# Where two pairs of modulation products and a table load stand in the norm transitions of a two-layer hybrid transformer

## The reference, cut to what matters

```python
def _rmsnorm(x, g):
    y = xf * lax.rsqrt(jnp.mean(xf * xf, axis=-1, keepdims=True) + EPS)
    return (y * g.astype(jnp.float32)).astype(x.dtype)

def _adaln(cond, w, b):
    return (jax.nn.silu(cond) @ w + b).reshape(cond.shape[0], 3 * N_SUB, D_MODEL)

def _modulate(x, g, mod, j):
    return _rmsnorm(x, g) * (1 + mod[:, 3 * j + 1, None]) + mod[:, 3 * j, None]

def _ffn_half(h, mod, j, g, w1, w3, w2):
    u = _modulate(h, g, mod, j)
    return h + 0.5 * mod[:, 3 * j + 2, None] * ((jax.nn.silu(u @ w1) * (u @ w3)) @ w2)
```

## Time and profile before

| what | us |
|---|---|
| median of 3 runs (lowest, highest) | 3353.94 (3353.17, 3354.42) |
| the profiled execution | 3349.25 |
| its span, first to last instruction | 3347.5 |
| PE busy in the span | 3190.4 (95%) |
| DVE busy | 1740.0 (52%) |
| ACT busy | 1406.5 (42%) |
| POOL busy | 124.1 (4%) |

### The profile page before, as it was taken

One profiled execution on the slowest core, in us unless ns is written; L12 is line 12 of the kernel. 1 busy time (PEld: TensorE's weight loads), 2 busy tenths in 40 slices (PEclk: granted clock), 3 DMA queues, 4 the chain that ended last, 5 costly groups with the idle time before them and its releaser, 6 DMA issues.

```text
span 3347.5 us, 51456 instructions
## 1 busy us (share of the span) xinstructions
PE 3190.4 (95%) x18766; PEld 2651.3 (79%) x18766; DVE 1740.0 (52%) x3164; ACT 1406.5 (42%) x2189; POOL 124.1 (4%) x120
## 2 busy tenths in 40 slices
PE   7999989999989899999999999999999998899898
PEld 4777768888877578777788867777788888699898
DVE  4333357777634823434333343334677775856555
ACT  4222256565434722224222242223655654654544
POOL 0000010111000000000000000000000000000000
PEclk9999999999999999999999999999899999999999
DMA  7443421111122043222432243434111113144454
GB/s 285 149 152 127 159 87 64 38 56 44 45 82 82 1 145 120 88 94 97 162 104 97 97 148 132 169 132 155 60 50 50 56 51 117 54 147 164 155 183 145
DMA packets 101261, 363.43 MB, mean 109 GB/s; under 512 B 11153, under 2 KB 12817, under 8 KB 101009
## 3 DMA queue, kind: packets, MB, share of 16 engines
q1 hardware_dynamic: 98384, 353.02, 30.9%
q10 hardware_dynamic: 2752, 8.72, 0.7%
HBM read 360.58 MB, written 1.11 MB: 108 GB/s over the span
## 4 chain that ended last, share of the span: by engine, by line
PE 85%; DVE 7%; ACT 4%; issue 3%; DMA 1%; SPq 0%; DVEq 0%; POOL 0%; POOLq 0%; ACTq 0%
PE bank L1662 67%; PE bank L1919 3%; PE bank L1917 2%; DVE wlo L1013 2%; PE bank L1687 2%; ACT whi L490 1%; PE bank L1970 1%; ACT scr L932 1%; PE bank L1978 1%; DVE h L1113 1%; PE bank L1988 1%; PE bank L1990 1%; PE bank L2125 1%; PE bank L2148 1%; PE bank L1960 1%
## 5 line engine op out<-in xcount | busy, mean ns | idle before, releaser
L1662 PE MATMUL bank<-uh,whi 128*128 128x512 f32 (+1 forms) x3008 | 1118.0, 372 | 52.9 <-ACTq L890 17.0
L1662 PE MATMUL bank<-ul,whi 128*128 128x512 f32 (+1 forms) x3008 | 1084.5, 361 | 0.0
L1662 PE MATMUL bank<-uh,wlo 128*128 128x512 f32 (+1 forms) x3008 | 1082.8, 360 | 0.5 <-DVE scr L1403 0.3
L490 ACT ACTIVATE whi<-raw 128x1024 fp32r<-128x1024 f32 x520 | 548.2, 1056 | 1209.3 <-PE bank L1662 1208.9
L1013 DVE TENSOR_TENSOR wlo<-raw,whi 128x1024 fp32r<-128x1024 f32 x520 | 642.4, 1235 | 790.5 <-ACT whi L490 789.2
L1662 PEld LDWEIGHTS bank<-uh,whi 128*128 128x128 f32 x3008 | 578.2, 192 | 160.5 <-issue 63.8
L1662 PEld LDWEIGHTS bank<-uh,wlo 128*128 128x128 f32 x3008 | 576.5, 192 | 81.8 <-DVE scr L1403 1.6
L1662 PEld LDWEIGHTS bank<-ul,whi 128*128 128x128 f32 x3008 | 578.7, 192 | 69.8 <-issue 2.2
L1662 PE MATMUL bank<-bh,whi 128*128 128x512 f32 (+1 forms) x1088 | 387.9, 357 | 1.1 <-DVE h L1113 0.8
L1662 PE MATMUL bank<-bl,whi 128*128 128x512 f32 (+1 forms) x1088 | 384.5, 353 | 0.0
L1662 PE MATMUL bank<-bh,wlo 128*128 128x512 f32 (+1 forms) x1088 | 384.4, 353 | 0.0
(11 more groups left out here) (247 smaller groups left out, 3041.3 us busy)
## 6 DMA issues: line engine op xcount, KB each, us to landing
raw<-stream SPq DMA_DIRECT2D x524, 512.0 KB, 3.3
ada_raw<-stream SPq DMA_DIRECT2D x131, 512.0 KB, 5.2
gc_row<-gc_rows ACTq DMA_DIRECT2D x16, 512.0 KB, 3.6
h<-h_in SPq DMA_DIRECT2D x1, 2048.0 KB, 10.9
m<-stream SPq DMA_DIRECT2D x4, 512.0 KB, 12.4
cst<-consts SPq DMA_DIRECT2D x1, 1104.0 KB, 12.5
scr<-stream SPq DMA_DIRECT2D x2, 512.0 KB, 16.2
out<-m SPq DMA_DIRECT2D x8, 128.0 KB, 1.8
```

Source lines behind the costliest of these rows:

```text
L490: act.activation(whi[:, j, :], raw[:, j, :], ACT.Copy).then_inc(hi_ready, 1)
L1662: last = mm(bank[j][:, c0:T], w(t, a), x[:, t, c0:T], start=n == 0, stop=n == 3 * kts - 1)
```

## The change

TensorE: in `last_products` the first pair of the leading group is issued behind panel (1, 1), the second of the last four, and the second pair between `sums_but_last` and `sum_last` instead of behind it. ScalarE: in transitions 1 to 6 the table load is issued before the wait for the residual of tile 7 and its square, instead of behind that square and the last weight split. SyncE: the load of the second pair of a leading group follows the raw load of panel 1 of its block, not of panel 2 (except for the first group, whose place is unchanged).

```diff
             if lead:
-                free = (max(b + 1, 1), 2 + k)
+                free = (b + 1, 1 + 2 * k) if b else (1, 2 + k)
             else:
                 free = (b + 2, 2 * k)
...
             def norm_rstd(n):
                 c0 = norm_conds(n)
-                log_exp()
+                if n == 0:
+                    log_exp()
                 act.wait_ge(var_ready, n + 1)
                 rsqrt(nrs[:, c0:T], nvar[:, c0:T], rstd_ready)
...
                 for i in range(2):
                     for j in range(4):
                         t = 4 * i + j
+                        if t == KT - 1:
+                            log_exp()
                         if j % 2:
                             have(act, pair_done[j // 2], G0 + i + 1)
                         else:
...
             def last_products(B0, G0, n, xh, xl, c0, kts=KT, ready=None, tile=None):
 
+                after = lead_after(n)
                 for i in range(2):
                     for j in range(4):
...
                         pair_free(G0 + i, j)
                         panel(B0 + i, j, xh, xl, c0, kts=kts, ready=ready if (i, j) == (0, 0) else None)
+                        if after is not None and (i, j) == (1, 1):
+                            ada_pair(after, 0)
                 sums_but_last(n)
-                after = lead_after(n)
-                if after is not None:
-                    ada_pair(after, 0)
-                sum_last(n)
                 if after is not None:
                     ada_pair(after, 1)
+                sum_last(n)
```

## The result

| | before | after |
|---|---|---|
| median of 22 runs (lowest, highest) | 3353.04 (3347.92, 3355.99) | 3356.98 (3355.27, 3360.58) |
| the profiled execution | 3349.25 | 3359.12 |
| its span | 3347.5 | 3357.3 |
| PE busy | 3190.4 (95%) | 3192.2 (95%) |

The ratio of the times is 1.0015, with a 95% interval of 1.0009 to 1.0022: slower by 5.0 (3.0 to 7.4). The medians lie only 3.9 apart, the means of the 22 runs each (3352.1 and 3357.2) 5.1: the runs of before fall into two groups, nine of 3347.9 to 3350.7 and thirteen of 3352.3 to 3356.0, and what parts them was not looked into. Forecast was +4.1. In the code of after the lines stand three further down: `panel` is L1665, the pair L1690, the first sum L1711, the last sum L1717, the variance L1033.

A forecast was written before the change was run, and what follows sets the result against it. The prediction took TensorE as the bound (85% of the span ends on it), time being lost where it stands still or another engines' chain sets its next matmul. 5.2 + 1.0 - 2.1 = +4.1, 3358.0 by the median; range 3351 to 3363.

The forecast's parts named there:

- the likeliest case: Transitions 1, 3, 4: last sum waits for the second pair's weights; forecast +4.1, anywhere up to +5.3, chance 0.67.
- Table load, 2.1 saved: ScalarE, load ahead of the last Square: Ln sooner by 0.31 in transitions 1, 3, 4, 0.16 in 2, 1.01 in 5.
- No cost in transition 6: Square there ends 0.44 later, hidden since the last sum waits behind the first; 0.1 to spare, at most 0.44 otherwise.
- First pair, +1.0 in transition 2 only: TensorE, behind the second of the last four panels: 1.0 added in transition 2, hidden in 1, 3, 4 with 0.1 to spare.
- Second pair, +5.2 for the late last sum: Pair between the sums waits for its loads: last sum +1.9 in transitions 1 and 3, +1.4 in 4, no wait in 2.
- the bound by rows 4: Lower bound: second slot takes 4.11 as in transition 2 before, so transition 1's last sum is on time within 0.1.
- The comparison of distances: Transition 1: the second half ought to start 6.2 earlier, and its load request moves by only 4.25.
- rival (b): Low clock behind the last sum lasts 3.4 longer, first panels lose up to 1.7 each; +7.5 with two transitions; chance 0.14.
- its condition: The clock rival decides from two of transitions 1, 2 and 3 on, with the low level 3.4 longer.
- the prediction's own sign of being wrong: In the profile after: a low clock much longer than 7 in transitions 1 to 3.
- (a): Second pair's loads arrive in time, as the 4.11 of transition 2 suggests, so -1.1 in all: 3352.8; chance 0.14.
- (c): ScalarE: a Square or weight copy restores the old table, Ln needs a second load, 1.28 in six transitions; +13.9; chance 0.02.

The follow-up runs named there:

- e2: The changed kernel with the table load put back behind the last Square, so the pairs alone are moved; 3357.07, ratio 1.0010 against the kernel before.
- e9: The changed kernel plus matmuls of constants behind the last sum (six in transitions 1 to 4, three in 5); 3353.20, ratio 1.0001 against before.
- e1: The kernel before with the table load alone moved ahead of the last Square; 3351.42 against 3353.85, ratio 0.9994.
- e6: e3 with both pairs back at their old places in transition 2; 3352.06, ratio 0.9997 against the kernel before.
- e3: The changed kernel with the second pair's load issued behind the raw load of panel 0 instead of panel 1; 3352.82, ratio 0.9999 against before.
- e4: The changed kernel with the second pair put back behind the last sum, its load staying in the new place; 3353.40, ratio 0.9999 against before.
- e7: The changed kernel with the second pair's load put back behind the raw load of panel 2; 3378.35 against 3352.18 before, ratio 1.0081.
- e8: e6 plus matmuls of constants behind the last sum (two in transition 2, six in 1, 3, 4, four in 5); 3346.34, ratio 0.9984 against before.
- e5: e3 plus matmuls of constants behind the last sum (six in transitions 1 to 4, four in 5); 3349.10, ratio 0.9991 against before.

## Why the prediction was right

The forecast was +4.1, the ratio says +5.0 (3.0 to 7.4), and the likeliest case took place: the second pair waited for its weights and the last sum for the pair. That the number comes so close is in part luck. The wait itself differs between executions of the same order: summed over transitions 1, 3 and 4 the last sum is 5.0 later than before in the profile of the changed kernel, 3.8 in that of e2 and 5.9 in that of e9. And the sum had no term for the slow last sums. By its steps:

- **Table load, 2.1 saved.** The distances of e1 give 1.9 up to the first ul, and 1.1 up to the first panel, as the late pair of transition 1 stands in the way there. In 1 to 4 the terms were exact (0.33, 0.16, 0.31, 0.31 for 0.31, 0.16, 0.31, 0.31). Transition 5 was 0.81 for 1.01. Ln did start 1.01 sooner, but VectorE had put a weight split into the time, and the scaling now waits for it:
```profile
3148.66 0.42 DVE L1033 TENSOR_SCALAR scr<-bank 128x256 f32<-128x256 f32 x1 [1.40 <-PE bank L1717]
3149.00 1.22 DVE L1016 TENSOR_TENSOR wlo<-raw,whi 128x1024 fp32r<-128x1024 f32 x1
...
3150.22 0.75 DVE L1065 TENSOR_TENSOR m<-h,scr 128x256 f32<-128x256 f32 x2
```
  The step did not ask what is late next behind Ln. (These rows are of after, transition 5.)
- **No cost in transition 6.** The Square starts behind the load, 0.97 behind the start of the residual instead of 0.52, and that is hidden almost wholly: from the residual of tile 7 to Ln it is 2.63 for 2.58. The first sum, which waits for POOL, is the cover, as predicted:
```profile
3347.33 1.28 ACT L494 ACT_TABLE_LOAD   x1
...
3348.60 0.70 PE L1711 MATMUL bank<-scr,cst 128*128 128x256 f32 x2 [0.98 <-POOL scr L450]
3348.63 0.42 ACT L524 ACTIVATE scr<-h 128x256 f32<-128x256 f32 x1
```
  The Square follows the load's end (3348.61) by 0.02. So the trace shows no drain behind the load at this place either, where the Trainium skill (ScalarE: Activation LUTs, "What ACT_TABLE_LOAD costs") has about 1.38 on top: the measurement decides, and the prediction's choice against it held. Nor is there one ahead of the load: in transition 1 it starts at 436.73, and the weight split before it ends at 436.71.
- **First pair, +1.0 in transition 2 only.** The place was right. The size was 1.27 (e6: 1.26): besides the pair's own 1.0 it starts 0.32 behind the matmul ahead of it, and the next ones start 0.34 and then 0.23 to 0.24 apart, instead of 0.227. In transition 1 the cover was as predicted, and nearly used up: the first sum's matmuls, idle for 1.10 before, now follow at once, its weight load still waits 0.26 for POOL, and the residual of tile 7 has no idle time.
- **Second pair, +5.2 for the late last sum.** Measured 1.41 + 2.15 + 1.46 = 5.02 (predicted 1.9 + 1.9 + 1.4), none in transition 2. e3, e4 and e7 show that it is the weights. The second load is used 5.4 after it goes out in transition 1 (435.18, 440.56), where the sum took 5.95: that term was too long there, and the bound by rows 4, 4.11, too short. The comparison of distances held: the slot is needed 6.2 earlier, and its request moved by 4.29, for 4.25 predicted.
- **What the sum did not have.** The last sum itself slower: +0.70 in transition 1, where the clock falls to 1.2 GHz within it, +0.95 in 3, where it had fallen, +0.16 in 5: 1.8. The prediction let the clock matter only for the panels behind the wait, in rival (b), and not for the sum that the wait holds up. With it: 5.02 + 1.8 + 1.27 for the first pair, less 2.13 for Ln, plus 0.19 for VectorE in transition 5 is 6.2, what the distances above give.
- **Rival (b), the clock,** came partly true in the profiled execution: the low level lasted 3.4 longer in transition 1 and 6.7 longer in 3, which meets its condition, two of the transitions 1 to 3, and the prediction's own sign of being wrong, but 3.5 less in 4. Its time, +7.5, was not reached. The mean granted clock of the 22 runs, 0.982, is not below that of before beside e2, 0.980, so the low level didn't last longer in all.
- **What the clock is worth** shows in the kernels with added matmuls: e8 is 5.7 below e6, and e9 and the changed kernel lie 0.0014 apart, 0 being just outside; the 0.0008 between e5 and e3 is inside the intervals.
- **Rivals (a) and (c)** are out: the loads were not in time, and no second table load stands in any transition.

What stays open: in the profiled pair some 1.7 beyond the start's 2.0 and the transitions' 6.2 is not placed. The panels behind the first one fall back by 1.1, 0.9 and 0.5 in transitions 2, 3 and 5 and not in 1 and 4; that is more than the 1.7, and where the rest is given back was not followed.

## What to carry to other kernels

When a consumer is moved forward, ask whether its DMA's request moves as far; work out both distances in the trace, and where the request can't follow, put the consumer behind the instruction that everybody waits for, not ahead of it. Here a load one panel earlier showed no cost and brought the ratio from 1.0015 back to 0.9999. When a stall is removed, look at each engine that used it for other work (here VectorE's weight split), and where TensorE has to stand still before a burst of matmuls, a few matmuls on constants that are sure to end in time can be worth more than a reordering (e8 against e6: 5.7).

## What the runs showed of the hardware that was not expected

- In transitions 1 and 3 of the changed kernel the granted clock fell in or right behind the wait in front of the sum, so the matmuls that end the stall are the slow ones: 1.13 became 1.83 and 2.07 for the same two matmuls, after TensorE had stood still but for two times eight small matmuls.
- Six calls (twelve instructions) of 384 columns in the wait held the granted clock at 1.00 for a stretch that had 0.66 without them. The Trainium skill (TensorE: Matmul & The Clock Gate, the part on the clock gate) warns of idle gaps between bursts of matmuls. e5 and e8 show what filling them is worth here, ratios of 0.9991 and 0.9984.
- A group of sixteen fp32 matmuls of 256 columns in a stream of fp32r matmuls costs more than its own 1.0: 1.26 to 1.27, as it starts 0.32 behind the matmul ahead of it and the first one behind it is followed after 0.34, for 0.227 elsewhere.
- The second 512 KB load of a pair was used 5.4 after it went out where a raw load had gone out 0.85 ahead of it (transition 1 of the changed kernel), and 4.1 after where that had gone 3.3 before.
